# Scan decays from one selecting product per head and direction, with the last adaptive tiles woven into the scan's preamble

## The reference, cut to what matters

```python
def ssd_chunked(xs, dt, a, bm, cm, h0):
    a_cum = jnp.cumsum((dt * a).reshape(b, nc, SSD_CHUNK, nh), axis=2)
    ...
    seg = a_cum[:, :, :, None, :] - a_cum[:, :, None, :, :]
    decay_ls = jnp.exp(jnp.where(causal[None, None, :, :, None], seg, -jnp.inf))
    scores = jnp.einsum("bclhn,bcshn->bclsh", cc, bc) * decay_ls
    y_diag = jnp.einsum("bclsh,bcshp->bclhp", scores, xdt)
    ...
# mixer_output: run once forwards (decays a[0]) and once on the flipped sequence (a[1]), and summed
# ada_mod:      m = jax.nn.silu(cvec) @ w_ada + b_ada      (six vectors of 1024 for each layer)
```

## Time and profile before

| what | value |
|---|---|
| median of 3 runs | 2557.5 us (2547.1 to 2561.46) |
| profiled execution | 2556.97 us, its span 2555.3 us |
| mean granted TensorE clock | 0.927 of full speed |
| PE busy | 2199.8 us, 86% |
| PE weight loads | 1933.2 us, 76% (beside the matmuls) |
| DVE busy | 1588.1 us, 62% |
| ACT busy | 1111.8 us, 44% |
| POOL busy | 474.7 us, 19% |
| chain that ended last | PE 42%, DVE 6%, ACT 2% |

### The profile page before, as it was taken

The page is one execution under the profiler, slowest core; times in us unless marked ns, Lnnn a source line. Parts: engine busy times, 40 slices in busy tenths (PEclk is TensorE's granted clock), DMA queues, the critical chain, the costliest instruction groups (busy, mean ns, idle before and its releaser), DMA issues.

```text
span 2555.3 us, 40376 instructions
## 1 busy us (share of the span) xinstructions
PE 2199.8 (86%) x15366; PEld 1933.2 (76%) x15376; DVE 1588.1 (62%) x2534; ACT 1111.8 (44%) x1624; POOL 474.7 (19%) x328
## 2 busy tenths in 40 slices
PE   5999887688589775876889999889997999899997
PEld 2776565677377565765868999779996999878997
DVE  2876654477468455765555776576667666546665
ACT  3223443576433544674445455224332433445332
POOL 1000001688400015884052021100000000000000
PEclk7998997899789887998999999989998999999999
DMA  6458611799445036996424466455553345323452
GB/s 249 165 205 320 216 58 63 274 344 347 181 148 199 32 116 215 326 322 223 134 98 181 167 217 225 158 196 188 184 186 132 139 174 205 132 100 116 173 186 85
DMA packets 103174, 471.50 MB, mean 185 GB/s; under 512 B 11520, under 2 KB 30208, under 8 KB 66048
## 3 DMA queue, kind: packets, MB, share of 16 engines
q1 hardware_dynamic: 84480, 404.79, 44.7%
q0 software_dynamic: 13232, 44.84, 4.7%
q10 hardware_dynamic: 5328, 20.07, 1.9%
HBM read 412.76 MB, written 54.79 MB: 183 GB/s over the span
## 4 chain that ended last, share of the span: by engine, by line
PE 42%; DVE 6%; ACT 2%; issue 1%; DVEq 1%; SPq 1%; DMA 0%; POOL 0%; ACTq 0%; POOLq 0%
PE bank L749 12%; PE bank L751 12%; PE bank L750 12%; DVE ring_halves L419 2%; ACT high L1402 1%; PE bank L1257 1%; PE bank L1121 1%; PE bank L1234 1%; PE bank L1247 1%; PE bank L1309 1%; PE bank L1290 1%; PE bank L1239 1%; PE bank L800 0%; DVE dring_halves L428 0%; PE bank L1238 0%
## 5 line engine op out<-in xcount | busy, mean ns | idle before, releaser
L749 PE MATMUL bank<-ssdb_halves,high 128*128 128x256 f32 (+1 forms) x2080 | 620.8, 298 | 49.1 <-DVE HT_halves L1934 18.4
L750 PE MATMUL bank<-HT_halves,high 128*128 128x256 f32 (+1 forms) x2096 | 621.9, 297 | 0.0
L751 PE MATMUL bank<-ssdb_halves,ring_halves 128*128 128x256 f32 (+1 forms) x2080 | 618.4, 297 | 0.0
L419 DVE TENSOR_TENSOR ring_halves<-ring,high 128x2048 fp32r<-128x2048 f32 (+1 forms) x230 | 482.3, 2098 | 195.9 <-ACT high L1402 194.3
L1402 ACT CAST high<-ring 128x2048 fp32r<-128x2048 f32 x230 | 437.3, 1903 | 218.5 <-PE bank L751 120.9
L749 PEld LDWEIGHTS bank<-ssdb_halves,high 128*128 128x128 f32 x2080 | 397.8, 191 | 68.6 <-issue 37.7
L750 PEld LDWEIGHTS bank<-HT_halves,high 128*128 128x128 f32 x2096 | 403.3, 192 | 8.9
L751 PEld LDWEIGHTS bank<-ssdb_halves,ring_halves 128*128 128x128 f32 x2080 | 398.2, 191 | 10.1
L419 POOL TENSOR_TENSOR ring_halves<-ring,high 128x1024 fp32r<-128x1024 f32 x66 | 224.7, 3405 | 674.9 <-ACT high L1402 674.9
L428 DVE TENSOR_TENSOR dring_halves<-dring,dhigh 128x1024 fp32r<-128x1024 f32 (+1 forms) x152 | 226.2, 1488 | 160.8 <-ACT dhigh L1408 160.3
L1408 ACT CAST dhigh<-dring 128x1024 fp32r<-128x1024 f32 x152 | 160.4, 1056 | 244.7 <-PE bank L751 244.6
(11 more groups left out here) (440 smaller groups left out, 3970.3 us busy)
## 6 DMA issues: line engine op xcount, KB each, us to landing
ring<-in_ffn SPq DMA_DIRECT2D x88, 1024.0 KB, 5.6
ring<-in_moe SPq DMA_DIRECT2D x64, 1024.0 KB, 7.3
ring<-in_ada SPq DMA_DIRECT2D x48, 1024.0 KB, 6.1
dring<-in_ffn_down SPq DMA_DIRECT2D x88, 512.0 KB, 3.6
dring<-in_moe_down SPq DMA_DIRECT2D x64, 512.0 KB, 4.6
ring<-in_foxin SPq DMA_DIRECT2D x24, 1024.0 KB, 4.9
ring<-in_win SPq DMA_DIRECT2D x22, 1024.0 KB, 8.0
zs_b<-x_slots POOLq DMA_DIRECT2D x32, 512.0 KB, 8.6
```

Source lines behind the costliest of these rows:

```text
L419: eng.tensor_tensor(low, w, h, ALU.subtract).then_inc(sem(f"low_{engine}"), 1)
L749: mm(o, a[0], b[0], start=first, stop=last and bool(kw), **kw)
L750: mm(o, a[0], b[1], start=False, stop=last and bool(kw), **kw)
L751: return mm(o, a[1], b[0], start=False, stop=last, **kw)
```

## The change

1. A head's decay sums come from one matmul for each direction. New code (`row_streams` says for which streams) forms on PE, once for a stream, the running sums of all heads as rows: `da_wide` (128 x 1024 for both streams, zeroed by DVE, heads written to columns 0 to 7 and again to 32 to 39 of each group of 128) is the stationary operand of 6 matmuls with 128 columns. ACT copies the 128 x 512 result into `da_rows`, every block of 128 twice (128 x 1024), rounded; DVE replaces the 8 rows from partition 32 by what the rounding left out (`sums`). `decay(h)` then multiplies `da_rows` by `sel`, a column of ones at the partitions h, 32 + h and so on, spread over 128 columns: 512 columns, one matmul a direction, and the mask.
2. PE's program after `win` is written in a new order. `ADA_STOPS` places the remaining adaptive tiles: between them come `x_tok` of stream 1 (now in banks 1 and 3), the rows, the sums `acum` of stream 1 (now in bank 4) and `ln_var`. `b_tok` of stream 1 goes to bank 1. `ssd(l, 1)` waits for the adaptive vectors only after `b_tok`.
3. ACT and DVE follow: ACT does its copies of stream 1, the rows, `end_decay` and the second group of SiLUs between the copies of the adaptive sums; DVE interleaves the steps of the second short convolution (`sconv(l, 1)`) with `steps`, `sums` and the rest, and makes `xw` (`weigh`) ahead of the adaptive vectors.

```diff
-ADA_SILU = 3
+ADA_STOPS = ((1, 4, 6, 8, 10), (1, 2, 3, 4, 4))
...
-        dar = sb("dar", [2, 4, 16])
+        sel = sb("sel", [HEADS])
...
+        da_rows, da_wide = view(HT_r[:].rearrange("p a b -> p (a b)"), 0, 2, 4 * T), view(HT[:].rearrange("p a b -> p (a b)"), 8 * T, 4, 2, P)
...
@@ PE, win @@
-                ada(l + 1, q0, 1)
+                stop = ADA_STOPS[l]
+                ada(l + 1, q0, stop[0])
                 narrow_turned(("win", l), 16, 3, 0, 2 * TB).then_inc(*done("dt_raw", l))
-                ada(l + 1, q0 + 1, ADA_PARTS[l + 1][-1] - q0)
+                ada(l + 1, q0 + stop[0], stop[1] - stop[0])
+                x_tok(l, 1, (1, 3))
+                ada(l + 1, q0 + stop[1], stop[2] - stop[1])
+                pe.wait_ge(*at("da", l))
+                for s in row_streams(l):
+                    rows, first, second = ps[2 - 2 * s], da_wide[:, 2 * s], da_wide[:, 2 * s + 1]
+                    mm(rows[:, 0:P], first[:, 0, :], up, start=True, stop=True)
+                    mm(rows[:, P:T], first[:, 0, :], one, start=True, stop=False)
+                    mm(rows[:, P:T], second[:, 0, :], up, start=False, stop=True)
+                    mm(rows[:, T:T + P], first[:, 1, :], lo, start=True, stop=False)
+                    mm(rows[:, T:T + P], second[:, 1, :], one, start=False, stop=True)
+                    mm(rows[:, T + P:2 * T], second[:, 1, :], lo, start=True, stop=True).then_inc(*done("s5_pe", ("rows", l, s)))
+                pe.wait_ge(*at("centred", l))
+                cum_sums(l, 1, ps[4])
+                ada(l + 1, q0 + stop[2], stop[3] - stop[2])
+                mean4(("ln_var", l), lambda c: sq[:, c, tok], 5, tok, lambda c: at("ln_sq", l))
+                ada(l + 1, q0 + stop[3], stop[4] - stop[3])
...
@@ PE, decay(h) @@
-                    for n in range(2):
-                        mm(f[:], r(dar[:, n, b0, h:h + 1]).to_broadcast([P, P]), r(fw), start=n == 0, stop=True, skip_group_check=True)
-                        mm(f[:, 2 * P:], r(dar[:, n, b1, h:h + 1]).to_broadcast([P, P]), r(fw[:, 0:2 * P]), start=False, stop=True, skip_group_check=True)
+                    one_row = lambda d: (r(sel[:, h:h + 1]).to_broadcast([P, P]), r(da_rows[:, s, 2 * d * T:2 * d * T + 2 * T]))
+                    mm(f[:], *one_row(0), start=True, stop=True, skip_group_check=True)
...
@@ ACT, after narrow @@
+                stop = ADA_STOPS[l]
+                ahead = 2 if l == 0 else 1
+                ada(l + 1, q, ahead)
+                if l == 0:
+                    ssd_in(l, 0)
+                ada(l + 1, q + ahead, 1)
+                softplus_log("dt", l, dts[:, 3, :, :], dts[:, 1, :, :])
+                ln_squares(l)
+                ada(l + 1, q + ahead + 1, stop[1] - ahead - 1)
+                for b in range(TB):
+                    act.wait_ge(*at("x_tok", (l, 1, b)))
+                    nc.scalar.copy(xtok[:, b, :], ps[1 + 2 * b][:]).then_inc(*done("x_tok_sb", (l, 1, b)))
+                ada(l + 1, q + stop[1], stop[2] - stop[1])
+                for s in row_streams(l):
+                    act.wait_ge(*at("s5_pe", ("rows", l, s)))
+                    nc.scalar.copy(r(da_rows[:, s, :]).rearrange("p (a m c) -> p a m c", a=4, m=2), twice(ps[2 - 2 * s][:])).then_inc(*done("s5_act", ("rows", l, s)))
+                act.wait_ge(*at("to_end", l))
+                act_fn(wst[:, 1, :, :], wst[:, 0, :, :], ACT.Exp).then_inc(*done("end_decay", l))
+                ada(l + 1, q + stop[2], stop[3] - stop[2])
+                ssd_in(l, 1)
+                ada(l + 1, q + stop[3], stop[4] - stop[3])
...
@@ DVE @@
                 dve.wait_ge(*at("dt_raw", l))
+                tss(da_wide[:].rearrange("p a b c -> p (a b) c"), ident.unsqueeze(1).to_broadcast([P, 8, P]), 0.0, ALU.mult)
...
+            def sums(l):
+
+                for s in row_streams(l):
+                    dve.wait_ge(*at("s5_act", ("rows", l, s)))
+                    own = da_rows[QUAD:QUAD + HEADS, s, :].rearrange("p (a m c) -> p a m c", a=4, m=2)
+                    tt(r(own), twice(ps[2 - 2 * s][QUAD:QUAD + HEADS, :], HEADS), own, ALU.subtract).then_inc(*done("s5_dve", ("rows", l, s)))
+                dve.wait_ge(*at("acum", (l, 1)))
...
@@ DVE, order of the program in layer 0 (else: layer 1) @@
+                second = sconv(l, 1)
+                if l == 0:
                     centre(l, streams * T)
                     steps_in(l)
+                    for _ in range(2):
+                        next(second)
+                    steps(l)
+                    for _ in range(2):
+                        next(second)
+                    sums(l)
+                    next(second)
                 else:
+                    for _ in range(4):
+                        next(second)
+                    steps_in(l)
                     centre(l, streams * T)
+                    next(second)
+                    steps(l)
+                    sums(l)
+                weigh(l)
                 ada(l + 1)
                 ssd(l, 1, not last)
...
+def row_streams(l):
+
+    return (1, 0) if l < DEPTH - 1 else (0,)
```

More of the change, by code:

```diff
@@ L791, in ada @@
                         mean_square(("mix", 0), slice(0, 2 * T))
-                if first + count == ADA_PARTS[part][-1] + 1:
+                if count and first + count == ADA_PARTS[part][-1] + 1:
                     ada_turned(first + count - 1)
@@ L891, in ssd, with x_tok @@
+                pe.wait_ge(*at("centred", l))
[3 more added lines that the diff above has]
+                ada(l + 1, q0 + stop[3], stop[4] - stop[3])
+            def x_tok(l, s, banks):
                 for b in range(TB):
+                    if s == 1 and b == 1:
+                        pe.wait_ge(*at("dt_abs", l))
                     for c in range(4):
@@ L898, in ssd, with cum_sums @@
-                for b in range(TB):
-                    for g in range(2):
-                        pe.wait_ge(*at("ssd_in", (l, 4 + g)))
-                        i = nc.tensor.transpose(ps[6][:, (2 * b + g) * P:(2 * b + g + 1) * P],
-                                                xs(4 + g)[:, o + b * P:o + b * P + P], ident)
-                i.then_inc(*done("b_tok", (l, s)))
-                pe.wait_ge(*at("da", l))
-                pe.wait_ge(*at("x_tok_sb", (l, s, 1)))
-                ac = ps[7]
+            def cum_sums(l, s, ac):
+                da, b0, b1 = dts[:, 5, :, :], 2 * s, 2 * s + 1
@@ L915, in ssd @@
                 mm(ac[:, 32:48], one, da[:, b1, :], start=False, stop=True).then_inc(*done("acum", (l, s)))
+            def ssd(l, s, full):
+                o = s * T
+                if s == 0:
+                    x_tok(l, 0, (6, 7))
+                pe.wait_ge(*at("x_tok_sb", (l, s, 0)))
+                for b in range(TB):
+                    for g in range(2):
+                        pe.wait_ge(*at("ssd_in", (l, 4 + g)))
+                        i = nc.tensor.transpose(ps[6 - 5 * s][:, (2 * b + g) * P:(2 * b + g + 1) * P],
+                                                xs(4 + g)[:, o + b * P:o + b * P + P], ident)
+                i.then_inc(*done("b_tok", (l, s)))
+                pe.wait_ge(*at("x_tok_sb", (l, s, 1)))
+                if s == 0:
+                    cum_sums(l, 0, ps[7])
+                else:
+                    pe.wait_ge(*at("s5_dve", ("ada", l + 1)))
                 if full:
@@ L924, in ssd @@
                 if s == 1:
-                    n = slice(0, 2 * T if full else T)
-                    mean4(("ln_var", l), lambda c: sq[:, c, n], 5, n, lambda c: at("ln_sq", l))
                     pe.wait_ge(*at("xw", l))
@@ L1532, in ssd @@
             def ssd(l, s, full):
-                for b in range(TB):
+                for b in range(TB) if s == 0 else ():
                     act.wait_ge(*at("x_tok", (l, s, b)))
@@ L1536, in ssd @@
                 act.wait_ge(*at("b_tok", (l, s)))
[L1537 removed]
+                nc.scalar.copy(btok[:].rearrange("p a b c -> p (a b c)"), ps[6 - 5 * s][:]).then_inc(*done("b_tok_sb", (l, s)))
                 if full:
@@ L1543, in ssd @@
                 if s == 1:
-                    act.wait_ge(*at("to_end", l))
-                    act_fn(wst[:, 1, :, :], wst[:, 0, :, :], ACT.Exp).then_inc(*done("end_decay", l))
                     for g in range(2):
@@ L1893, in _ @@
                 .then_inc(*done("tri_rounded"))
+            nc.vector.tensor_copy(r(sel[:]), k("fold32")[:, 0:HEADS])
             dve.wait_ge(sem("vec_loaded"), 32)
@@ L2126, in ssd @@
                 dt = dts[:, 4, :, :]
[L2127 to L2149 removed]
+                if s == 1 and not full:
+                    ln_rstd(l, T)
+                    ln_scale(l, T)
+                if not full:
+                    return
+                if s == 0:
+                    dve.wait_ge(*at("acum", (l, s)))
                     tss(nacum[:], ps[7][:, 0:32].rearrange("p (a b) -> p a b", a=2), -1.0, ALU.mult)\
                         .then_inc(*done("acum_sb", (l, s)))
```

88 lines of the change are left out of this document (29 added, 59 removed).

## The result

Five runs of the changed kernel took 2537.26 us in the median (2532.57 to 2540.45), beside 2555.36 us for five runs of the kernel before: a ratio of 0.9938, 95% interval 0.992 to 0.9955. A second measurement of the same two kernels gave 2533.3 us (6 runs) against 2554.35 (10 runs): 0.9913, 0.9893 to 0.9934. So the change makes the kernel some 0.6 to 0.9% faster; 2540 was forecast, inside the range of 2527 to 2554.

A forecast was written before the change was run, and what follows sets the result against it. PE was taken to bound the scans, with DVE next, and a chain the preamble. Scans 2.7 + 3.3 + 3.3, starts 3.5, preambles 2 + 3 make 17.8 us off 2556.97: 2539.2, stated as 2540, range 2527 to 2554.

The forecast's parts named there:

- the scans: Three scans: thinned decays let PE drop below DVE's pace, gaining 2.7 + 3.3 + 3.3 us, 9.3 in all.
- the starts: Stream 0 scan starts, both layers: a shorter first decay gains 3.5 us together, bounds 1.8 and 3.8.
- the preambles: Stretches ahead of the scans: the new order gains 2 us in layer 0 and 3 in layer 1.
- granted clock 1.00 there: Inside the scans: PE keeps its full clock; a clock under 1 would show the prediction wrong.
- the terms 2.7 and 3.3: Gains in us forecast for the scans of layer 0 stream 1 and layer 1 stream 0.
- The third rival: Scans: thinned PE work loses the fast clock, 37 us more, 2585 if it held for all heads; chance 0.07.
- under 2: Second scan's start: its first decay was to take under 2 us.
- case 1: The forecast itself: DVE-bound scans, clock partly low in the preambles, 2534 to 2547, centre 2540; chance 0.50.
- The term of 2: Layer 0 preamble: clock falls at about 229, returns on dense rows; states end at 260, gain 2 us.
- the term of 3: Layer 1 preamble: states end at 849, between 845 and 855, a gain of 3 us.
- the order gains nothing: Preambles: PE stays at the low clock and moved work is paid there, 2550 us; chance 0.26.
- Full clock in the preambles: Preambles at full clock gain 7.5 and 7 us instead of 2 and 3, giving 2530; chance 0.17.

The follow-up runs named there:

- early tables: Changed kernel with ACT's square root ahead of its `b_tok` copy and a one-element exponential ahead of the state copies: 2528.01 us, ratio 0.9906 of the kernel before.
- Order alone: Changed kernel's new order with the decays formed as before and no rows: 2539.64 us, ratio 0.9956 of the kernel before.
- all three edits: Changed kernel plus table loads moved into ACT's waits, DVE's negated sums before its scaling, ACT's adaptive copy before its squares: 2520.21 us, 0.9865 of before.
- filler: Changed kernel with ten extra selecting products while PE waits for ACT's table loads in layer 0 stream 1: 2529.77 us, ratio 0.9908 of the kernel before.
- the third move: ACT copies the fourth adaptive tile's sums before its squares; alone on the changed kernel: 2537.78 us, ratio 0.9937 of the kernel before.

## Why the prediction was right

**The total was partly luck.** 17.8 us were forecast and 16.5 measured in the first trace's span, but no group of terms came out as forecast: the scans gave 7.5 us instead of 9.3, the starts 4.5 instead of 3.5 (the bounds were 1.8 and 3.8), the preambles 7.0 instead of 5, and the untouched rest took 2.4. In the second pair of traces the spread is wider still. What was right is the mechanism of the parts: DVE is the bound of the thinned scans, the first decay of stream 0 shrinks, and the order gains.

**The scans.** PE's head came out as worked out (0.92 for 0.89, 1.92 for 1.90), and DVE is the bound behind it: 24.70 us where 24.5 to 25 was said, and 19.16 where 19.2 was said, in the one first scan that kept its clock. The step that failed is "granted clock 1.00 there". The prediction itself counts a clock under 1 in the scans as a sign that it is wrong, and on that point it is. It was 0.87 and 0.93 in two of the three scans, and the terms 2.7 and 3.3 measured 1.45 and 2.45; by the mean over the nine traces with new decays (20.5, 25.4, 25.7 us) the three scans gain 7.1 us, not 9.3.

**The third rival** was thus half right: the thinned scan does lose the fast clock. Its price was wrong. It stays low for the first one to three heads (267.44 to 270.87 is a head of 3.43 us instead of 1.92), and comes back while PE runs without gaps (3.40 of 3.40 us busy from 268.3 on), which is what the prediction held against the rival: 0.7 to 2 us a scan, not 37 in all. The Trainium skill, page "TensorE: Matmul & The Clock Gate", section "A second HAM failure mode: psum-queue depth-cycling", has the clock lost and regained over and over where PE pauses between groups of matmuls. In part the runs agree: 20 of 27 scans lose it, each time beside PE's pauses. In part they don't: a scan loses it once and not over and over, and the scan of stream 0 has the same pauses at its start (1.34 and 1.10 us) and kept 1.00 in the first trace.

**The starts.** 1.87 and 2.59 us, 4.46 together for 3.5, and above the bound of 3.8. The place was right: the first decay of stream 0 took 1.49 us ("under 2"), 1.76 less than before, and both starts hang on it. The excess is in layer 1, where the kernel before had a clock of 0.78 in the first trace; with the clock at 1.00 and 0.98 it gained 0.98, which is the 0.9 that the prediction gives for full clock. In layer 0 stream 1 nothing was to come, and nothing came, since ACT's loads fill that stretch; early tables shows that they are what fills it.

**The preambles.** The mechanism of case 1 (clock falls at about 229, comes back on dense rows) is what the trace shows: full clock to 229.6, low from 229.65, full again from about 236.6. Last turning 250.39 (247 to 252 was said), states 260.01 (under 262.0), wait for ACT 1.81 us (2 was said), rows 232.61 to 235.31, 2.70 us a stream at the low clock (2.8). The term of 2 measured 2.66, and 7.5 in the second pair of traces, where before had the low clock from 219.93 on. In layer 1 the term of 3 was short: 4.34 in the first pair and 8.7 in the second. It was worked out like layer 0's and left out the 5.87 us for which PE stood still before the change. Three of the four tiles and the rows ran at full clock, up to 823.7; the sums, the last tile and most of the variance did not. The other costs were within their bounds: zeroing 0.69 us (at most 1.21), subtraction 1.22 (1.21). In layer 0 PE never waited for them; in layer 1 it waited 1.40 us, at 822.24, for DVE's copy of the step sizes into `da_wide`, a wait that the prediction had not placed.

**The other rivals.** Order alone gives 11 us, so "the order gains nothing" is out. "Full clock in the preambles" (2530) did not hold in layer 0 of the changed kernel, but the median of its second measurement, 2533.3, lies between the two cases, and the trace with all three edits shows that clock up to the last turning.

**What stays open:** what decides whether the clock falls behind the same idle of 1.10 us. It differs between executions of one program, and a filler of 2.4 us did nothing to be seen. I could not set it apart from its timing.

## What to carry to other kernels

When PE sheds half of a loop's work, the gain ends where the next engine's own work begins: add up that engine's instructions from a stretch in which it doesn't wait, and expect to give a little of it back at the loop's first or last turns, where PE now has gaps. Then look at what the shorter loop leaves exposed in front of it. Here that was two table loads and one small instruction behind a long one; moving these by a few lines, with no work removed, was worth some 13 us together with the third move, beside 18 to 21 for the change itself. And in layer 1 a wait of 5.87 us of PE, for DVE and behind it for ACT, was there to be read before the change: look at PE's waits in each layer, and not at one layer for both.

Before a stage of two single traces is compared, profile one kernel twice. The old scans, with the clock at 1.00, repeated to 0.02 us; the stretches around a fall of the clock moved by up to 6.

## What the runs showed of the hardware

The clock can fall in a stretch in one execution and not in the next of the same program: the way from layer 1's mean to the scan took 38.76 and 32.54 us, the second scan ran at 1.00 and at 0.92. Two executions of the changed kernel that were profiled, in separate measurements, differ by 18 us, as much as the change is worth; the six of the second measurement alone lie within 14 us.

A table load takes 1.28 us whether or not anything waits for it, and an exponential of a single element (0.20 us) pulls it forward into a wait. The Trainium skill, page "ScalarE activation tables: per-element evaluation and per-set limits", section "What a function is on this engine", states that two functions in different sets are one load apart and gives the same duration, 1283 ns; by the traces, that is the whole price, also right behind another instruction: 260.65 to 261.94 behind a copy, 262.65 to 263.94 behind the square root.
